# Attention in two layers: weights requested a block earlier, set-ups waited for one by one, the turned key in other banks

## The reference

```python
def mla_q(cq, q_norm_w, w_uq, q_head_norm_w, cos, sin):
    q = (rms_norm(cq, q_norm_w) @ w_uq).reshape(B, T, MLA_HEADS, MLA_QK)
    q = rms_norm(q, q_head_norm_w)
    if cos is not None:
        q = jnp.concatenate([q[..., :MLA_NOPE], apply_rope(q[..., MLA_NOPE:], cos, sin)], axis=-1)
    return q

def mla_kv(ckv, kr, kv_norm_w, w_ukv, k_head_norm_w, cos, sin):
    kv = (rms_norm(ckv, kv_norm_w) @ w_ukv).reshape(B, T, MLA_HEADS, MLA_NOPE + MLA_V)
    k_rope = jnp.broadcast_to(kr[:, :, None, :], (B, T, MLA_HEADS, MLA_ROPE))
    k = rms_norm(jnp.concatenate([k_nope, k_rope], axis=-1), k_head_norm_w)
    ...

def attend(q, k, v):
    s = jnp.einsum('bqhd,bkhd->bhqk', qi, k).astype(jnp.float32) * sm_scale
    p = jax.nn.softmax(s, axis=-1).astype(v.dtype)
    return jnp.einsum('bhqk,bkhd->bqhd', p, v)
```

## Time and profile before

| | us |
|---|---|
| median of 3 runs | 4681.37 |
| lowest, highest | 4678.23, 4686.35 |
| profiled execution | 4673.74 |
| its span | 4671.9 |
| attention's block, layer 1: first request, last gating | 490.20, 998.17 |
| attention's block, layer 2: first request | 1543.05 |

### The profile page before, as it was taken

How to read it: one execution, slowest core, us unless ns; L and a number is a source line. 1 busy time by engine, 2 the same in 40 slices (tenths; PEclk the granted TensorE clock), 3 DMA queues, 4 the chain that set the end, 5 groups by cost and what they waited for, 6 DMA issues and landing times. The chain is left out here.

```text
span 4671.9 us, 43111 instructions
## 1 busy us (share of the span) xinstructions
PE 3918.0 (84%) x16125; PEld 2801.0 (60%) x16125; DVE 2227.5 (48%) x2705; ACT 1443.0 (31%) x2378; POOL 940.3 (20%) x408
## 2 busy tenths in 40 slices
PE   5998699979598699986866899887999855999995
PEld 2786355557486355564634776565877644666663
DVE  5563466641392467632437426433122113666665
ACT  3111355530211354422041335222110012555541
POOL 1342200012252200021411011244344321000001
PEclk7999699989799799988988999998999966999997
DMA  5110122222111111122211110111221234999994
GB/s 216 32 37 25 25 81 81 81 93 99 34 45 30 25 54 59 63 72 73 40 46 40 36 39 14 30 25 27 47 47 41 72 110 138 379 380 380 380 347 177
DMA packets 337557, 470.08 MB, mean 101 GB/s; under 512 B 46317, under 2 KB 201186, under 8 KB 335842
## 3 DMA queue, kind: packets, MB, share of 16 engines
q1 hardware_dynamic: 324594, 423.10, 27.8%
q0 software_dynamic: 7888, 26.78, 1.6%
q10 hardware_dynamic: 4896, 17.83, 0.9%
HBM read 395.81 MB, written 71.86 MB: 100 GB/s over the span
## 5 line engine op out<-in xcount | busy, mean ns | idle before, releaser
L1180 PE MATMUL values<-probs,vp 128*128 128x512 f32 x672 | 348.9, 601 | 12.1 <-issue 6.4
L1464 POOL TENSOR_TENSOR out_hi<-out_w,ones 128x1024 fp32r<-128x1024 f32 x24 | 71.3, 2972 | 1158.7 <-DMA out_w<-in_w_out 1158.7
L1269 ACT ACTIVATE probs<-scores 128x512 f32<-128x512 f32 (+1 forms) x336 | 196.0, 583 | 309.3 <-PE scores L404 307.6
L402 PE MATMUL scores<-q_hi,k_rest 97*128 97x512 f32 (+1 forms) x336 | 262.7, 782 | 0.0
L767 DVE SCALAR_TENSOR_TENSOR conv_out<-conv_in,vectors,conv_out 128x1295 f32<-128x1295 f32 (+1 forms) x120 | 254.1, 2118 | 4.3
L3284 PE MATMUL dp<-h_t,abt 128*128 128x512 f32 x544 | 241.9, 597 | 3.1 <-ACT abt L3335 3.1
L402 PE MATMUL gates_ps<-x_t_r,gates_w_r 128*128 128x512 f32 (+1 forms) x560 | 210.5, 376 | 23.1 <-POOL gates_w_r L450 23.1
L3317 ACT ACTIVATE expert_hi<-wu 128x1024 fp32r<-128x1024 f32 x136 | 144.8, 1064 | 245.1 <-PE gp L404 245.1
L1351 DVE TENSOR_REDUCE mx<-made 128x1 f32<-128x640 f32 (+1 forms) x272 | 203.7, 793 | 27.0 <-PE made L1121 26.3
L402 PE MATMUL out_ps<-h_t_r,out_w_r 128*128 128x512 f32 (+1 forms) x448 | 171.4, 383 | 46.8 <-POOL out_w_r L1466 46.8
L403 PE MATMUL gates_ps<-h_t_r,gates_hi 128*128 128x512 f32 (+1 forms) x560 | 209.8, 375 | 0.0
(11 more groups left out here) (556 smaller groups left out, 9701.5 us busy)
## 6 DMA issues: line engine op xcount, KB each, us to landing
wg<-in_w_gate SPq DMA_DIRECT2D x34, 2048.0 KB, 10.4
wu<-in_w_up SPq DMA_DIRECT2D x34, 2048.0 KB, 11.8
h_t<-in_w_down SPq DMA_DIRECT2D x34, 2048.0 KB, 10.4
slot_rows<-zero_rows SPq DMA_DIRECT2D x16, 1536.0 KB, 9.7
...
```

Source lines behind the costliest of these rows:

```text
L402: nc.tensor.matmul(out, lhs[1], rhs[0], start=start, stop=False, **kw)
L1180: nc.tensor.matmul(O[b % 2][:, 0:w], vp[g // 2 % 2][:, kb, g % 2 * VD:g % 2 * VD + P], pr[m % 3][:, 0:w], start=kb == 0, stop=kb == nk - 1 ...
L1269: nc.scalar.activation(pr[m % 3][:, 0:w], S[m % 2][:, 0:w], ACT.Exp, scale=scale).then_inc(s.exped, 1)
L1464: nc.gpsimd.tensor_tensor(hi[:, c, :, :], wt[:, c, :, :], all_ones(k), ALU.mult).then_inc(s.split, 1)
```

## The change

The loads of the heads' weights, with their tiles and semaphores, move from `attention` into a new `attention_weights`; they are requested by SyncE in the norms' block, and the tiles and the semaphores live until the end of the layer. The key is spread into the banks `S[0]`, `S[1]` and `O[0]` (scores and values) instead of `made`. GpSimd's chain is put in another order, and each user waits for the count at which its piece is set. TensorE waits for the squared and the turned key only ahead of the first key's sum of squares and of the first score.

```diff
+def attention_weights(nc, k, a, l, es):
+    t = es.enter_context(stage(nc, "k_in sel_in q_in rope_in"))
...
+    def loads(sp):
+        sp.dma_start(t.sel[:, :], a.sel).then_inc(t.sel_in, 16)
+        sp.dma_start(t.wkv[:, :, :], a.w_ukv[l].rearrange("p (h n) -> p h n", h=HEADS)).then_inc(t.k_in, 16)
+        sp.dma_start(t.table[NOPE:P, :], a.rope[NOPE:P, :]).then_inc(t.rope_in, 16)
+            for c in range(2):
+                sp.dma_start(t.wq[:, c, :, 0:QK], w_uq[:, c, :, :]).then_inc(t.q_in, 16)
...
-def norm_groups(nc, k, items):
+def norm_groups(nc, k, items, loads=None):
...
+        if loads:
+            @block.sync
+            def _(sp):
+                loads(sp)
...
-        ONCE = 11
+        KR = [S[0], S[1], O[0]]
+        MAX_SET, VALUES_SET, ROWS_SET, SUMS_SET, ROWS_1_SET, ZERO_SET = 1, 3, 6, 7, 10, 11
...
-                        sp.wait_ge(s.set_once, ONCE)
+                        sp.wait_ge(s.set_once, ZERO_SET)
...
-            for i in range(2):
+            def rows(i):
                 for row, value in ((k_hi, 1.0), (k_rest, 0.0), (q_rest, 0.0)):
                     once(nc.gpsimd.tensor_scalar(row[i][QK:QK + 1, :], one, value, None, ALU.mult))
             once(nc.gpsimd.memset(mx[:, :, :], -1e30))
             for i in range(2):
                 once(nc.gpsimd.memset(vp[i][:, :, VD:2 * VD], 1.0))
+            rows(0)
             once(nc.gpsimd.memset(acc[:, :], 0.0))
+            rows(1)
...
+                if g == 0 and i == first_k:
+                    pe.wait_ge(s.kr_squared, 3)
...
+                    if g < 2:
+                        pe.wait_ge(s.set_once, ROWS_1_SET if g else ROWS_SET)
+                if m == 0:
+                    pe.wait_ge(s.kr_squared, 3)
+                    pe.wait_ge(s.krope_made, 3)
...
-                nc.tensor.matmul(J[:, b, 0:w], sel[:, :], kr[:, t0:t0 + w], start=True, stop=True).then_inc(s.kr_made, 1)
-            pe.wait_ge(s.k_in, 16)
-            pe.wait_ge(s.kr_squared, 3)
-            pe.wait_ge(s.krope_made, 3)
-            pe.wait_ge(s.set_once, ONCE - 1)
+                nc.tensor.matmul(KR[b][:, 0:w], sel[:, :], kr[:, t0:t0 + w], start=True, stop=True).then_inc(s.kr_made, 1)
+            pe.wait_ge(heads.k_in, 16)
...
-            act.wait_ge(s.set_once, ONCE - 1)
...
-                if g and m == 0:
-                    dve.wait_ge(s.combined, g)
+                if m == 0:
+                    dve.wait_ge(s.combined, g) if g else dve.wait_ge(s.set_once, MAX_SET)
...
+                else:
+                    dve.wait_ge(s.set_once, SUMS_SET)
...
             dve.wait_ge(s.krope_made, 3)
-            dve.wait_ge(s.set_once, ONCE - 1)
```

57 lines of the change are left out of this document (30 added, 27 removed).

## The result

| | before | after |
|---|---|---|
| median of the runs, us | 4683.86 (4 runs) | 4647.15 (4 runs) |
| lowest, highest | 4678.23, 4687.41 | 4636.21, 4649.18 |
| span of the profiled execution | 4671.9 | 4647.4 |

The ratio is 0.9918, with a 95% interval from 0.9899 to 0.9937: 36.7 us less by the medians, where 38.8 were forecast.

What follows compares the result with a forecast made beforehand. Mostly TensorE (84%), with the winnable time its idle wait on GpSimd at attention's opening: 19.7 + 20.4 - 1.3 = 38.8 us, off an expected median of 4681.4, gives 4642.6 us; range 4630 to 4657 us.

Steps and rivals of the forecast that it cites:

- What bounds the kernel: Opening of attention: TensorE idles 20.44 and 21.84 us before the first query projection, at a gate until GpSimd clears sums.
- (a): Heads' weights requested one block earlier, in the norms: costed at nothing; loads left in place would delay the projection 9 us.
- (b): Opening of attention: first projection waits for neither key nor GpSimd; step-by-step timing gives gains of 19.7 and 20.4 us.
- the uncertain input: Whether GpSimd's clear blocks VectorE operations with two SBUF inputs: taken as no, 40.1 us; if yes, 32.6 us.
- the cold variant: Opening of attention with TensorE at 1.2 GHz for the whole preparation: gains of 16.3 and 17.7 us.
- the warm course: Opening of attention with TensorE's clock rising within 10 us of its start: gains of 19.7 and 20.4 us.
- (c): One wait on GpSimd became several in attention, each for a piece set long before: costed at nothing.
- (d): One more semaphore group closed with a barrier behind attention's last block, 0.64 us a layer: 1.3 us charged.
- A: Opening of attention: GpSimd's row set-ups hold VectorE little or not at all; gain 50.7 us, 4631 us; chance 0.17.
- B: Opening of attention: two-SBUF-input operations stay behind the whole set-up chain; gain 13.8 us, 4668 us; chance 0.09.
- C: Behind the opening of attention, a wait takes the gain back; 4681 us; chance 0.05.
- D: Heads of attention entered at a lower TensorE clock, making the kernel slower; one whole head gives 4697 us; chance 0.03.

Runs made afterwards that it cites:

- the profile with the pause: Kernel before plus one VectorE wait, ahead of its second block of subtractions behind attention, until GpSimd has rounded the first weights: 4670.82 us, ratio 0.9964.

## Why the prediction was right, point by point

**What bounds the kernel** held: the gate is the gain. With it back in place the time is that of before within 0.2%.

**(a) The loads**: nothing comes late, as forecast. SyncE issued the first and the last of them in the norms' block:

```profile
473.21 0.34 SPq L902 DMA_DIRECT2D sel<-in_sel  x1
...
480.94 0.87 SPq L909 DMA_DIRECT2D wq<-in_w_uq  x1
```

The last is out 11 us before the projection wants it. What they would cost in their old place was put at 9 us at the projection; it was 7, in a single run, and 4.6 of them reach the maxima.

**(b) The walk** was right in its mechanism. GpSimd's timeline in layer 1, the six row set-ups and the clear between them:

```profile
489.99 3.48 POOL L1089 TENSOR_SCALAR k_hi<-ones 1x1280 fp32r<-1x1280 f32 x1
493.55 3.98 POOL L1089 TENSOR_SCALAR k_rest<-ones 1x1280 fp32r<-1x1280 f32 x1
497.61 3.44 POOL L1089 TENSOR_SCALAR q_rest<-ones 1x1280 fp32r<-1x1280 f32 x1
501.11 5.22 POOL L1095 MEMSET ahead_sums<- 128x6144 f32 x1
506.41 3.44 POOL L1089 TENSOR_SCALAR k_hi<-ones 1x1280 fp32r<-1x1280 f32 x1
509.94 3.44 POOL L1089 TENSOR_SCALAR k_rest<-ones 1x1280 fp32r<-1x1280 f32 x1
513.46 3.44 POOL L1089 TENSOR_SCALAR q_rest<-ones 1x1280 fp32r<-1x1280 f32 x1
```

And VectorE beside it: the two additions of the key, the addition of q0 in the clear, its rest, the addition and product of q1, and the key's scaling.

```profile
493.54 0.68 DVE L1435 TENSOR_TENSOR krope<-krope,turned 32x512 f32<-32x512 f32 x1
...
495.88 1.74 DVE L1435 TENSOR_TENSOR krope<-krope,turned 32x512 f32<-32x512 f32 x1
...
503.25 0.68 DVE L1359 TENSOR_TENSOR qt<-qt,turned 32x512 f32<-32x512 f32 x1
...
506.42 3.53 DVE L1366 TENSOR_TENSOR q_rest<-qt,q_hi 96x512 fp32r<-96x512 f32 x1 [1.78 <-ACT q_hi L1257]
...
512.29 1.18 DVE L1359 TENSOR_TENSOR qt<-qt,turned 32x512 f32<-32x512 f32 x1
513.51 3.49 DVE L1360 TENSOR_TENSOR qt<-qt,rs 32x512 f32<-32x512 f32 x1
...
518.30 0.47 DVE L1343 SCALAR_TENSOR_TENSOR kt<-made,vectors,rs 64x256 f32<-64x256 f32 x1
```

The operations with two SBUF inputs that meet a row set-up end just behind it: 512.29 + 1.18 is 513.47, and the fifth set-up ends at 513.38. Inside the clear they keep their 0.68 us. This was the uncertain input on which the sum was taken to be 40.1 and not 32.6 us; the trace decides it for the clear that blocks no one, and the kernel with the clear at the end shows it once more. The rule of the Trainium skill, SBUF — State Buffer, section "Who interferes with whom", whose second half no row of before could show, agrees with both.

Layer 2 came out as walked. The rows of q1 there, each ending with the fourth, fifth and sixth set-up:

```profile
1547.41 2.95 DVE L1359 TENSOR_TENSOR qt<-qt,turned 32x512 f32<-32x512 f32 x1
1550.39 3.49 DVE L1360 TENSOR_TENSOR qt<-qt,rs 32x512 f32<-32x512 f32 x1
...
1554.58 2.83 DVE L1366 TENSOR_TENSOR q_rest<-qt,q_hi 96x512 fp32r<-96x512 f32 x1 [0.70 <-ACT q_hi L1257]
```

The maxima start at 35.0 us behind the block, where 35 was forecast: 20.5 us gained, 20.4 forecast. Layer 1 took the cold variant, 39.9 us where it had 39.7: 16.2 gained, 16.3 forecast. The windows show the clock, two for each layer, the key's matmuls and what follows (PEclk is the number behind POOL's):

```profile
488.00:491.00 3.00, 2.57 (x4) 1.49 (x5) 0.48 (x1) 1.97 (x3) 2.39 (x4) 0.54 0.52 150
...
493.00:500.00 7.00, 6.32 (x8) 2.21 (x8) 4.43 (x5) 1.69 (x3) 6.83 (x3) 0.50 0.01 3
...
1529.00:1532.00 3.00, 2.93 (x5) 1.62 (x6) 0.48 (x1) 2.19 (x4) 2.77 (x4) 0.55 0.63 193
...
1535.00:1540.00 5.00, 4.32 (x9) 1.34 (x7) 3.01 (x4) 1.90 (x3) 4.92 (x2) 0.89 0.00 0
```

In layer 1 the clock fell 0.2 us ahead of the block's start, in layer 2 0.3 us behind it (by the means of 0.54 and 0.55 over 3 us). In layer 2 it rose again 7.1 us behind the start, in layer 1 at 13.5 us. In layer 1 q0's rest was therefore issued 18.0 us behind the start instead of 15.4 and missed the clear: it came at 506.42, 0.01 us behind the start of the fourth set-up, and lasted 3.53 us. The prediction has the clock fall during the wait on GpSimd; in the trace of before it had fallen 1.4 us behind the block's start in layer 1 and 0.2 us ahead of it in layer 2, before the key's matmuls ran. The forecast took the warm course for both layers. In the two profiles it was one warm and one colder opening each, 36.6 and 37.6 us together instead of 40.1. That is the term which was too large, by 2.5 to 3.5 us. From the key's first scaling to the maxima the walk had 8.2 us in layer 1; it was 10.0 and 7.8 in the two profiles, and 6.7 and 8.2 in layer 2, where it had 7.0.

Two details of the walk were wrong without moving the sum. The key's additions were put behind the second and the third set-up, since the walk let them start only when all squares were there; VectorE takes block after block, and they ended at 5.8 and 9.2 us instead of 8.8 and 12.3. The first scaling therefore waits for the root of the projection (12.5 us), not for the key, and the number 12.3 was right by accident. And the first of them wasn't held at all: it started 0.01 us ahead of the second set-up, which took 3.98 us instead of 3.44 in its place.

**(c)** None of the finer waits appears in the trace: nobody waits for `set_once` behind the block's start.

**(d) The seam** was put at 0.64 us a layer. From VectorE's last sum of the modulation to ScalarE's first rounding, before and after, in layer 1:

```profile
1019.49 0.27 DVE L527 TENSOR_TENSOR mod<-ahead_ps,vectors 128x24 f32<-128x24 f32 x2 [21.32 <-PE ahead_ps L519]
...
1020.40 0.72 ACT L1493 ACTIVATE h_t_r<-branches 128x256 fp32r<-128x256 f32 x2 [24.27 <-PEq L81]
```
```profile
1001.96 0.27 DVE L527 TENSOR_TENSOR mod<-ahead_ps,vectors 128x24 f32<-128x24 f32 x2 [21.31 <-PE ahead_ps L519]
...
1003.63 0.72 ACT L1522 ACTIVATE h_t_r<-branches 128x256 fp32r<-128x256 f32 x2 [25.02 <-PEq L81]
```

From 0.91 to 1.67 us: 0.76 us. In layer 2 it goes from 0.96 to 1.28 us, 0.32 more, and so it does in every profile with the change. That is 1.1 us in both layers, forecast 1.3.

**The sum**: 36.6 or 37.6 us from the openings less 1.1 is 35.5 to 36.5 us, forecast 38.8; the medians give 36.7 in the first set of runs and 44.2 in the second, and the gate put back against the change 0.9991 to 0.9918, some 34 us. The kernel before varies too: its layer 1 had 57.3 instead of 56.0 in the profile with the pause, which lies behind that opening. So the mechanism and its size in the openings are borne out; that the first median came within 2.1 us of the forecast is partly luck, since the two sets of runs differ by 7.5 us. **The base**: the profiled execution of before had the quick course of the stage behind attention in layer 2 and the shortest tail of all profiles, so the two profiles differ by 24.5 us only. Setting the gain against the median, 7.6 us above that profile, was the right choice, made without my knowing where they lay.

**The rivals.** A (no lock) falls by the blocked operations. What it says of the lock's price was near: the forecast put the lock at 5.8 and 6.1 us (25.5 and 26.5 against 19.7 and 20.4), and the rows by memset, which shorten the chain as well, took off 6.4 and 5.3 at the same clock, 3.7 at another. No kernel with that edit alone reached the 30 us of rival A: they had 31.7 to 33.5, with the lower clock at the start. B falls by the operations that got through at each boundary, C by the table of stretches (nothing takes the gain back in attention; what is lost behind it lies in stages that the diff doesn't touch), D by the heads: from the maxima to the stage behind they took 475.4 and 449.3 us, 474.2 and 448.7 before, so the colder entry didn't reach them.
